# One wide operand in the gated up projections, a three-term output projection of the latent heads, GpSimd's rests in pieces, and a last expert by columns

## The reference

```python
# each layer i of the first block
o_na  = neighborhood_attention(...)          # 8 heads of 64: (256, 512)
o_mla = latent_attention(...)                # 8 heads of 64: (256, 512)
merged = sigmoid(g_na + b) * (o_na @ w_na_o[i]) + sigmoid(g_mla + b) * (o_mla @ w_mla_o[i])
x = layer_norm(ALPHA * x + merged @ w_out[i])
if i == 0: f = (silu(x @ ffn_w1) * (x @ ffn_w3)) @ ffn_w2           # hidden width 2816
else:      f = mixture of 8 experts, top 2, same form, hidden width 3584
x = layer_norm(ALPHA * x + f + sigmoid(x @ w_ple_gate[i]) * (p[i] @ w_ple[i]))
# end of the second block
return x + (silu(h2 @ w_gate) * (h2 @ w_up)) @ w_down                # hidden width 2816
```

## Time and profile before

| what | value |
|---|---|
| median of 3 runs (lowest, highest) | 2028.69 us (2028.56, 2030.53) |
| the profiled execution, its own time | 2030.13 us |
| its span, first to last instruction | 2028.3 us |
| busy TensorE | 1990.2 us, 98% |
| busy VectorE | 1535.9 us, 76% |
| busy ScalarE | 1012.3 us, 50% |
| busy GpSimd | 79.9 us, 4% |
| mean granted TensorE clock | 0.996 |

### The profile page before, as it was taken

How to read it: one execution, slowest core, us unless ns; L and a number is a source line. 1 busy time by engine, 2 the same in 40 slices (tenths; PEclk the granted TensorE clock), 3 DMA queues, 4 the chain that set the end, 5 groups by cost and what they waited for, 6 DMA issues and landing times.

```text
span 2028.3 us, 28426 instructions
## 1 busy us (share of the span) xinstructions
PE 1990.2 (98%) x11368; PEld 1714.6 (85%) x11368; DVE 1535.9 (76%) x1541; ACT 1012.3 (50%) x1064; POOL 79.9 (4%) x57
## 2 busy tenths in 40 slices
PE   8999999999999989999999999999999998999999
PEld 8988799989988778888888888888888877869998
DVE  3674677776654698888888888888888976567766
ACT  0363110011452377777777777777777753472000
POOL 0111100000001200000000000000001000100000
PEclk9999999999999999999999999999999999999999
DMA  9643588744634689999999999999999984435550
GB/s 328 197 152 110 184 297 307 270 148 129 218 125 151 235 297 384 381 379 371 385 385 375 385 381 380 370 384 385 377 384 380 408 284 151 145 105 178 196 176 33
DMA packets 184221, 553.22 MB, mean 273 GB/s; under 512 B 9296, under 2 KB 112080, under 8 KB 140864
## 3 DMA queue, kind: packets, MB, share of 16 engines
q1 hardware_dynamic: 175296, 517.55, 69.7%
q10 hardware_dynamic: 6912, 25.02, 3.0%
q0 software_dynamic: 1920, 9.34, 1.2%
HBM read 528.02 MB, written 23.59 MB: 272 GB/s over the span
## 4 chain that ended last, share of the span: by engine, by line
PE 95%; DVE 3%; ACT 2%; issue 1%; DMA 0%; DVEq 0%; ACTq 0%; SPq 0%
PE act_ps L1168 29%; PE dve_ps L1193 15%; PE act_ps L1029 15%; PE dve_ps L1029 9%; PE job_ps L1123 6%; PE dve_ps L905 6%; PE act_ps L1076 2%; PE job_ps L1056 2%; PE act_ps L905 1%; PE job_ps L1176 1%; PE job_ps L956 1%; PE job_ps L998 1%; PE job_ps L984 1%; PE act_ps L1455 1%; PE act_ps L1301 1%
## 5 line engine op out<-in xcount | busy, mean ns | idle before, releaser
L2388 DVE TENSOR_TENSOR weights_rest<-weight_ring,expert_short 128x2048 fp32r<-128x2048 f32 x336 | 763.0, 2290 | 103.1 <-ACT expert_short L1720 102.5
L1720 ACT ACTIVATE expert_short<-weight_ring 128x2048 fp32r<-128x2048 f32 x336 | 641.1, 1916 | 109.8 <-PE act_ps L1168 74.0
L1168 PE MATMUL act_ps<-expert_short,tokens_short 128*128 128x512 f32 x896 | 354.2, 395 | 4.0 <-ACT arena_o L1737 2.1
L1168 PE MATMUL act_ps<-expert_short,tokens_rest 128*128 128x512 f32 x896 | 349.2, 390 | 0.0
L1168 PE MATMUL act_ps<-weights_rest,tokens_short 128*128 128x512 f32 x896 | 349.1, 390 | 0.0
L1628 ACT ACTIVATE arena_mla<-act_ps 128x256 f32<-128x256 f32 (+1 forms) x72 | 31.0, 432 | 377.3 <-PE act_ps L1029 335.8
L1168 PEld LDWEIGHTS act_ps<-expert_short,tokens_short 128*128 128x128 f32 x896 | 168.2, 188 | 38.7 <-DVE weights_rest L2388 3.2
L1168 PEld LDWEIGHTS act_ps<-expert_short,tokens_rest 128*128 128x128 f32 x896 | 168.2, 188 | 36.2
L1168 PEld LDWEIGHTS act_ps<-weights_rest,tokens_short 128*128 128x128 f32 x896 | 168.4, 188 | 33.6
L2317 DVE TENSOR_TENSOR weights_rest<-weight_ring,ffn_weights_short 128x2048 fp32r<-128x2048 f32 x66 | 151.3, 2292 | 2.2
L1193 PE MATMUL dve_ps<-expert_short,hidden_short 128*128 128x512 f32 x448 | 139.5, 393 | 0.0
(11 more groups left out here) (408 smaller groups left out, 3721.1 us busy)
## 6 DMA issues: line engine op xcount, KB each, us to landing
weight_ring<-in_moe_w SPq DMA_DIRECT2D x336, 1024.0 KB, 7.0
weight_ring<-in_w_in SPq DMA_DIRECT2D x43, 1024.0 KB, 8.0
weight_ring<-in_ffn_w SPq DMA_DIRECT2D x32, 1024.0 KB, 7.6
weight_ring<-in_w_out SPq DMA_DIRECT2D x12, 1024.0 KB, 6.4
weight_ring<-in_w_gate SPq DMA_DIRECT2D x11, 1024.0 KB, 5.5
weight_ring<-in_w_up SPq DMA_DIRECT2D x11, 1024.0 KB, 8.0
weight_ring<-in_w_down SPq DMA_DIRECT2D x10, 1024.0 KB, 7.0
weight_ring<-in_w_ple_gate SPq DMA_DIRECT2D x8, 1024.0 KB, 6.5
```

The source lines that it names most:

```text
L1168: m = nc.tensor.matmul(bank[0:CAP, :], a[:, 4 * c + k, :], w[:, k, :], start=(c == k == i == 0), stop=(c == 1 and k == 3 and i == 2))
L1720: nc.scalar.activation(shorts[u % SHORTS][:, :], ring[:, slot, half], ACT.Copy).then_inc(moe_w_short, 1)
L2388: V.tensor_tensor(ring_lo[slot][:, half], ring[:, slot, half], shorts[u % SHORTS][:, :], ALU.subtract)\
```

## The change

It does five things.

1. In both gated feed-forwards the short and the rest of the input are read as one operand of 512 columns. For each step there is one matmul of the short weights with both (512 wide, into the whole bank), and one of the rest of the weights with the short input (256 wide, into the first half of the bank). VectorE then adds the two halves of a bank with a reduction over two elements, for w1 tiles too, which ScalarE read before. Silu and the multiplication work on pairs of tiles in SBUF, and the split of the unit two ahead comes before the split of the hidden pair.
2. The `o_mla` projection runs in three terms of fp32r instead of plain fp32. ScalarE makes the short weights (two casts of 2048) between its sigmoids and its small copy; VectorE makes the short and rest of `o_mla` (1024 each) behind the second `o_na` tile and the rests of the weights (2048 each) behind the third and the fifth.
3. The last attention output is copied behind the second `o_na` tile instead of ahead of the first.
4. Each of GpSimd's three subtractions per layer is issued as four of 512.
5. The last expert's last down pair is done by column halves: 12 matmuls for the first half, then 12 for the second. Behind four of the second 12, the first half's two products (banks 0 and 2) are put in; the other two (banks 1 and 3) end it. ScalarE does both copies. VectorE takes the banks in the order 0, 2, 1, 3.

Cut to its core:

```diff
+PUT_ORDER = (0, 2, 1, 3)
+PUT_BEHIND = 4
+        o_x = [parts("heads_short", "probs", [P, 4, SEQ]), parts("heads_rest", "probs", [P, 4, SEQ], 4 * SEQ)]
+        ff_x_both = parts("ffn_in_both", "work", [P, 6, DT * SEQ])[:, 0:6:5, :]
+        ff_up = std[:, :, :].rearrange("p t s -> p (t s)")
...
@@ block.gpsimd
-                    nc.gpsimd.tensor_tensor(ring_lo[block % RING][:, half], ring[:, block % RING, half], ff_w[i % 2][:, :],
-                                            ALU.subtract).then_inc(pool_w_split, 1)
+                    for piece in range(POOL_PIECES):
+                        at = slice(c * 2048 + 512 * piece, c * 2048 + 512 * (piece + 1))
+                        nc.gpsimd.tensor_tensor(ring_lo[block % RING][:, at], ring[:, block % RING, at],
+                                                ff_w[i % 2][:, 512 * piece:512 * (piece + 1)], ALU.subtract).then_inc(pool_w_split, 1)
...
@@ block.tensor
+            def half_terms(bank, w, at, k):
+                short, rest = w
+                both = ff_x_both[:, :, k * SEQ:(k + 1) * SEQ]
+                if k:
+                    nc.tensor.matmul(bank[:, 0:SEQ], rest[:, k, at], ff_x[0][:, k, :], start=False, stop=True, skip_group_check=True)
+                m = nc.tensor.matmul(tiles(bank[:, :], 2), short[:, k, at], both, start=k == 0, stop=True,
+                                     skip_group_check=k > 0)
+                if k == 0:
+                    nc.tensor.matmul(bank[:, 0:SEQ], rest[:, k, at], ff_x[0][:, k, :], start=False, stop=True, skip_group_check=True)
+                return m
...
-                            m = split_product(bank[:, 0:SEQ], (short, rest), at, ff_x)
+                            for k in range(DT):
+                                m = half_terms(bank, (short, rest), at, k)
...
-                for c in range(2):
-                    down(it, GROUPS_E - 1, c)
-                pe.wait_ge(put_ready, turn + 1)
-                for b in range(4):
...
+                def put_back(columns):
+                    pe.wait_ge(last_y[columns], turn + 1)
+                    for b in PUT_ORDER[2 * columns:2 * columns + 2]:
+                        nc.tensor.matmul(acc_ps[b][:, :], put_gate[0:CAP, b // 2 * P:(b // 2 + 1) * P],
+                                         moe_y[0:CAP, columns * 512:(columns + 1) * 512], start=True, stop=True).then_inc(last_scattered, 1)
+                for columns in range(2):
...
+                                if columns == 1 and done == PUT_BEHIND:
+                                    pe.wait_ge(put_ready, turn + 1)
+                                    put_back(0)
+                                m = nc.tensor.matmul(dve_ps[columns][0:CAP, :], h[:, g % 2, 2 * c + k, :],
+                                                     w[:, k, columns * 512:(columns + 1) * 512], start=False, stop=c == k == 1 and i == 2)
...
+                put_back(1)
...
-                heads_w.append(weights(4, D))
-                pe.wait_ge(out_copied, layer_pairs * (l + 1))
-                heads_tiles(o_mla, 0, DT)
+                pe.wait_ge(heads_split, l + 1)
+                for j in range(DT):
+                    bank, at = dve_bank(), slice(j * P, (j + 1) * P)
+                    for k in range(4):
+                        if j == 0 and k % 2 == 0:
+                            pe.wait_ge(heads_w_split, 2 * l + k // 2 + 1)
+                        short = tiles(in_w[k // 2][:, :], 2)[:, k % 2, at]
+                        for i, (w, o) in enumerate(((short, 0), (short, 1), (heads_rest[:, k, at], 0))):
+                            m = nc.tensor.matmul(bank[:, 0:SEQ], w, o_x[o][:, k, :], start=(k == i == 0), stop=(k == 3 and i == 2))
+                    m.then_inc(dve_tile_ready, 1)
@@ block.scalar
-                    read(ff_silu[:, f // 2 % 2, f % 2 * SEQ:(f % 2 + 1) * SEQ], ACT.Silu)
+                    n.a += 2
+                    act.wait_ge(act_tile_done, n.a)
+                    h = ff_silu[:, pair % 2, :]
+                    nc.scalar.activation(h, h, ACT.Silu).then_inc(ffn_silu_done, 1)
...
+                act.wait_ge(*weights_landed(heads_block))
+                for c in range(2):
+                    act.wait_ge(*in_units(l)[IN_UNITS - 2 + c][2])
+                    nc.scalar.activation(in_w[c][:, :], ring[:, heads_block % RING, c * 2048:(c + 1) * 2048], ACT.Copy)\
+                        .then_inc(heads_w_short, 1)
@@ block.vector
                     if kind == "w1":
+                        for j in range(2):
+                            bank = act_ready()
+                            V.tensor_reduce(h[:, j * SEQ:(j + 1) * SEQ], halves_of(bank), AX_X, ALU.add).then_inc(act_tile_done, 1)
                     elif kind == "w3":
-                            V.tensor_tensor(part, ready()[:, 0:SEQ], part, ALU.mult).then_inc(dve_tile_done, 1)
+                        for j in range(2):
+                            bank = ready()
+                            V.tensor_reduce(ff_up[:, j * SEQ:(j + 1) * SEQ], halves_of(bank), AX_X, ALU.add).then_inc(dve_tile_done, 1)
+                        dve.wait_ge(ffn_silu_done, n.pair)
+                        V.tensor_tensor(h, ff_up, h, ALU.mult).then_inc(ffn_h_full, 1)
+                    split_w(units, u + 2)
+                    if kind == "w3":
...
                         V.tensor_copy(short, h).then_inc(ffn_h_short, 1)
                         V.tensor_tensor(rest, h, short, ALU.subtract).then_inc(ffn_h_ready, 1)
-                    split_w(units, u + 2)
...
                 for j in range(DT):
                     V.tensor_tensor(merged[:, j, :], ready()[:, 0:SEQ], gates[0][:, j, :], ALU.mult).then_inc(dve_tile_done, 1)
+                    if j == 1:
+                        output(layer_pairs * (l + 1) - 1)
+                        V.tensor_copy(o_x[0][:, :, :], o_mla).then_inc(heads_short, 1)
+                        V.tensor_tensor(o_x[1][:, :, :], o_mla, o_x[0][:, :, :], ALU.subtract).then_inc(heads_split, 1)
+                    if j in (2, 4):
+                        heads_rest(j // 2 - 1)
```

More of the change, by code:

```diff
@@ L628, in build @@
         mix_w_parts = [in_w[0][:, :], in_w[1][:, :], in_x[0][:, :, :].rearrange("p t s -> p (t s)")]
+        POOL_PIECES = 4
         POOL_UNITS, DVE_UNITS = (0, 1, 5), (2, 3, 4, 6, 7)
@@ L1102, in first_gate_tiles @@
                     for j, bank in enumerate(banks):
-                        for i, (a, x_part) in enumerate(((w[0], 0), (w[0], 1), (w[1], 0))):
-                            m = nc.tensor.matmul(bank[:, 0:SEQ], a[:, k, j * P:(j + 1) * P], ff_x[x_part][:, k, :],
-                                                 start=(k == i == 0), stop=(k == DT - 1 and i == 2))
+                        m = half_terms(bank, w, slice(j * P, (j + 1) * P), k)
                         if k == DT - 1:
@@ L1241, in experts @@
                 one(it, last_beside)
-                for c in range(2):
-                    down(it, GROUPS_E - 1, c)
-                pe.wait_ge(put_ready, turn + 1)
-                for b in range(4):
-                    if b < 2:
-                        pe.wait_ge(last_y[b], turn + 1)
-                    nc.tensor.matmul(acc_ps[b][:, :], put_gate[0:CAP, b // 2 * P:(b // 2 + 1) * P],
-                                     moe_y[0:CAP, b % 2 * 512:(b % 2 + 1) * 512], start=True, stop=True).then_inc(last_scattered, 1)
+                def put_back(columns):
[3 more added lines that the diff above has]
+                                         moe_y[0:CAP, columns * 512:(columns + 1) * 512], start=True, stop=True).then_inc(last_scattered, 1)
+                g = GROUPS_E - 1
+                pe.wait_ge(moe_h_done, it * GROUPS_E + (g + 1))
+                for columns in range(2):
+                    done = 0
+                    for c in range(2):
+                        u = moe_unit_of("w2", g, c)
+                        slot, half = unit_half(u)
+                        if columns == 0:
+                            pe.wait_ge(*rest_ready(u, it))
+                        short, rest = tiles(shorts[u % SHORTS][:, :], 2), tiles(ring_lo[slot][:, half], 2)
+                        for k in range(2):
+                            for i, (h, w) in enumerate(((h_hi, short), (h_hi, rest), (h_lo, short))):
+                                if columns == 1 and done == PUT_BEHIND:
[3 more added lines that the diff above has]
+                                                     w[:, k, columns * 512:(columns + 1) * 512], start=False, stop=c == k == 1 and i == 2)
+                                done += 1
+                        if columns == 1:
+                            m.then_inc(moe_unit_done, 1)
+                    if columns == 0:
+                        m.then_inc(last_columns, 1)
+                put_back(1)
             pe.wait_ge(x_here[0], 16)
@@ L1699, in attention, with swiglu @@
                         fill(p)
-            def swiglu(f_tiles, clear=False):
-                for f in range(f_tiles):
```

(38 more changed lines are left out.)

68 lines of the change are left out of this document (41 added, 27 removed).

## The result

The changed kernel took 2019.60 us (median of 5 runs, 2019.06 to 2022.97) against 2028.69: a ratio of 0.995, 95% interval 0.9936 to 0.9964. Measured a second time, on another occasion, it was 2022.68 against 2029.81: 0.9969, interval 0.9957 to 0.9981. The forecast was 2017.3, its range 2013 to 2023. The profiled executions went from 2028.3 to 2017.4 us of span, 10.9 less, close to the 11.4 of the sum. The parts are not close to theirs, though, as the stages show.

The account below looks back on a forecast made before the run. TensorE, holding 95% of the chain of waits, was taken as the bound. Savings of 8.6 + 1.8 + 1.0 = 11.4 us brought the profiled 2030.13 to 2018.7, and, being 1.44 over the median, the forecast to 2017.3, range 2013 to 2023.

Parts of the forecast that it names:

- the sum: Whole kernel: 8.6 us from the feed-forwards, 1.8 from two layers' heads stages and 1.0 behind the last expert, 11.4 saved.
- Wide operand, TensorE: Feed-forwards' w1 and w3 units: a step falls from 360 to 347.9 ns, over 704 steps 8.6 us saved.
- Wide operand, VectorE: Feed-forwards: VectorE's work per pair rises from about 9.0 to 11.13 us, nothing stalls and TensorE's 8.6 us arrive whole.
- The price of the reduction: Feed-forwards: VectorE adding the halves of a 512-element bank takes 0.68 us, taken from the nearest row.
- the tie: Feed-forwards: VectorE's pair of units and TensorE's pair both take 11.13 us.
- The lead: Feed-forwards: VectorE's split of the unit two ahead ends some 1.3 us before TensorE needs it.
- Heads: Heads stage, per layer: 0.79 + 2.44 - 0.63 = 2.6 us, less 1.7 of contention, gains 0.9 (-1.2 to 2.6).
- The contention: Heads' new tiles: VectorE waits 0.57 us per GpSimd piece, four pieces, less TensorE's lead of 0.55: 1.7 us lost per layer.
- rival (d): Heads: full blocking, each GpSimd piece holds one VectorE operation to its end; layers lose 2.4 us, total 2021.5; chance 0.10.
- Last expert: Last expert's down matmuls, copies and products: VectorE ends at 1677.3 in place of 1678.28, gain 1.0 us (0 to 2.8).
- Small moves: ScalarE's row-clearing transfers follow its Silu, and the last expert's slots come free up to 1.8 us later: no cost.
- unit 5: Unit beside a cut GpSimd subtraction: no gain, since ScalarE's bank copy lets TensorE go on, not the blocked cast.

## Why the prediction was right, point by point

The time came within the range, and in part by its width and by luck: the terms add up to 8.1 us instead of 11.4, and one of the three has the wrong sign. The first profile's 10.9 looked like a confirmation only because its clock was kinder.

**Wide operand, TensorE.** Right in kind, 7.4 instead of 8.6 us. The mis-sized term is the step: 349.7 ns where the forecast had 347.9, times 704 some 1.3 us. The forecast took both paces from streams of one kind; what makes the wide one longer in this stream is open.

**Wide operand, VectorE.** The price of the reduction (0.682 forecast, 0.685 measured), the pair (11.13 and 11.12) and the tie hold. The lead was too large, which mattered only when the load was raised.

**Heads.** The sum without contention (2.6) is what is measured without GpSimd (2.57). The contention was put at 1.7 and is 2.09, so 0.48 is left instead of 0.9. VectorE's four disturbed operations waited some 3.3 us in all (1.40, 1.06, 1.38 and 1.05 less 0.42 or 0.28): 0.84 apiece, not the 0.57 that the forecast took. The mechanism is that of rival (d), each piece holding one operation to its end; it costs less than (d)'s 1.09 apiece because the operations meet a piece under way. TensorE loses 2.09 of the 3.3, so by difference its lead soaks up 1.3 and not 0.55. That GpSimd's pieces are the condition for any gain here the forecast did not say: it set their worth at the waits, without pricing a whole subtraction or the clock behind a long pause. It is 4.1 us per layer, and without pieces the change as a whole is worth nothing.

**Last expert.** This step failed. The forecast followed copies, products and VectorE to 1677.3 and stopped at the aggregate; those 0.9 us were there. (By its own terms, 1674.1 and 2.9, the end is 1677.0 and the gain 1.3; measured are 0.96.) It did not ask how long TensorE needs from its last product to the transposes. That time had been covered by VectorE's work; with that work earlier, it ends last, and the gain of 1.0 is a loss of 0.3.

**Small moves, unit 5.** Costed at nothing, and the stage with unit 5 is 31.34 and 31.35.

**The sum.** 8.1 us of the kernel's own in place of 11.4; the profiled span hid this, as the granted clock was kinder to the first changed profile by 2.8. Both medians, 2019.60 and 2022.68, stood within the range; the second is above the 2015 to 2020 of the forecast. The prediction had also put the clock aside, its mean being 0.996; two short stretches of it made 2.8 us between the first two profiles, more than the 0.96 of both heads stages.

## What to carry to other kernels

A gain worked out up to the last operation of a stage is not yet a gain: follow it to the first instruction of the next stage on the bounding engine, with what that engine has to get past on its way. Where VectorE reads two operands from SBUF, or casts, beside GpSimd, it can wait to the end of the GpSimd instruction; cutting that in four was worth 4.1 us per layer, of which 2.7 were the lower clock behind TensorE's pause of 3.4. And compare by stages, with a second profile of each kernel, before a difference of spans is shared out among the edits.

## What the runs showed of the hardware that was not expected

- Passing a block that is not entered can cost its engine some 4 us: TensorE's first transposes came 3.9 to 4.5 us behind its last product in ten profiles with the block, and 1.2 us earlier in the one without. VectorE stood 4.09 us between its copy and its addition in one kernel, less than 2.0 in another with the same lines.
- The granted clock after a pause of 6.4 us differs between executions of one kernel: 1.00 or 0.89 over 13 to 15 us that take in the end of the pause and what follows, 1.25 us of time.
- Behind a pause of 3.4 us in the heads stage the granted clock was 0.50 for some 6 us, in both layers; behind pauses of 0.58 and 1.03 us it stayed at 1.00.
- A 512-column fp32r matmul took 230 ns in the up projections and 226.7 in the down projections, and neither the alternation with narrow ones nor an operand in two places accounts for it (0.1 to 0.2 us of a stage at most).
